# One decoder step on one core: layer norm's roots in one group, linear attention by split operands, sample columns turned in one piece, h's sums two per tile

## The reference, cut to what matters

```
a_u, a_v = gelu(a_u), gelu(a_v)
vn = layernorm(a_v)                       # per token, over 1024 channels
s  = spatial_mix(vn, w_s, b_s)            # 128x128 lower triangle, per head of 128 channels, per chunk of 128 tokens
out_a = a_u * s * silu(a_z)
# linear attention, 4 heads, keys of 128, values of 256
scores = where(mask, q_dec @ k_dec.T, 0)
o  = scores @ v + q_dec @ S               # S: state carried from chunk to chunk
S  = exp(b_last) * S + k_scaled.T @ v
out_b = rmsnorm(o) * gn_g * silu(b_z)
out_c = softmax(c_q @ mk.T / 16) @ mv * silu(c_z)
x = x + (sum over the branches: sigmoid(gate) * (out @ w_branch)) @ w_out
```

## Time and profile before

| | us |
|---|---|
| median of 3 runs | 867.17 (866.44 to 868.7) |
| the profiled execution | 868.86 |
| its span, first to last instruction | 866.6 |
| TensorE busy | 853.5 |
| VectorE busy | 430.2 |
| ScalarE busy | 377.3 |
| GpSimd busy | 92.4 |

### The profile page before, as it was taken

The page is one execution under the profiler, slowest core; times in us unless marked ns, Lnnn a source line. Parts: engine busy times, 40 slices in busy tenths (PEclk is TensorE's granted clock), DMA queues, the critical chain, the costliest instruction groups (busy, mean ns, idle before and its releaser), DMA issues.

```text
span 866.6 us, 16310 instructions
## 1 busy us (share of the span) xinstructions
PE 853.5 (98%) x6931; PEld 829.1 (96%) x6931; DVE 430.2 (50%) x748; ACT 377.3 (44%) x596; POOL 92.4 (11%) x127
## 2 busy tenths in 40 slices
PE   8999999999999999999999999999999999999997
PEld 8999999999999999999999998999989999999995
DVE  6525642634454466323337788545343544445634
ACT  7534445247555442422232275333234544534424
POOL 1001000000000222101012158000110000000000
PEclk9999999999999999999999999999999999999999
DMA  8325743331322659623366861425563341252402
GB/s 294 80 88 167 256 146 98 96 102 49 116 80 86 212 194 338 218 72 113 135 219 227 309 194 52 145 99 194 195 243 98 99 132 64 98 193 78 143 2 98
DMA packets 86067, 126.10 MB, mean 146 GB/s; under 512 B 3058, under 2 KB 72736, under 8 KB 86000
## 3 DMA queue, kind: packets, MB, share of 16 engines
q1 hardware_dynamic: 72288, 76.58, 27.1%
q0 software_dynamic: 13616, 48.48, 16.0%
q10 hardware_dynamic: 96, 0.06, 0.0%
HBM read 112.91 MB, written 12.19 MB: 144 GB/s over the span
## 4 chain that ended last, share of the span: by engine, by line
PE 95%; DVE 2%; ACT 1%; DMA 1%; issue 1%; ACTq 0%; DVEq 0%
PE mm L1020 63%; PE mm L981 5%; PE mm L994 5%; PE mm L970 3%; PE mm L1304 2%; PE mm L1230 2%; PE p L955 1%; PE p L957 1%; PE p L956 1%; PE mm L1251 1%; PE mm L1250 1%; PE mm L1249 1%; PE p L1189 1%; PE p L1159 1%; PE p L1133 1%; PE p L1130 1%
## 5 line engine op out<-in xcount | busy, mean ns | idle before, releaser
L1020 PE MATMUL mm<-h_lo,w_hi 128*128 128x260 f32 (+1 forms) x1088 | 223.6, 287 | 2.0 <-DVE w_lo L1399 2.0
L1020 PE MATMUL mm<-h_hi,w_hi 128*128 128x260 f32 (+1 forms) x1088 | 219.6, 283 | 0.0
L1020 PE MATMUL mm<-h_hi,w_lo 128*128 128x260 f32 (+1 forms) x1088 | 218.9, 283 | 0.0
L1399 DVE TENSOR_TENSOR w_lo<-raw,w_hi 128x1024 fp32r<-128x1024 f32 x130 | 159.4, 1229 | 89.2 <-ACT w_hi L526 88.0
L1020 PEld LDWEIGHTS mm<-h_lo,w_hi 128*128 128x128 f32 x1088 | 168.6, 189 | 6.2 <-issue 3.3
L1020 PEld LDWEIGHTS mm<-h_hi,w_lo 128*128 128x128 f32 x1088 | 168.1, 189 | 0.0
L1020 PEld LDWEIGHTS mm<-h_hi,w_hi 128*128 128x128 f32 x1088 | 168.1, 189 | 0.0
L526 ACT ACTIVATE w_hi<-raw 128x1024 fp32r<-128x1024 f32 x130 | 135.8, 1052 | 13.9 <-DMA raw<-in_w_mem_kv_dram 5.1
L1020 PE MATMUL mm<-x_lo,w_hi 128*128 128x260 f32 (+1 forms) x448 | 96.2, 284 | 0.0
L1020 PE MATMUL mm<-x_hi,w_hi 128*128 128x260 f32 (+1 forms) x448 | 95.3, 283 | 0.0
L1020 PE MATMUL mm<-x_hi,w_lo 128*128 128x260 f32 (+1 forms) x448 | 95.1, 282 | 0.0
(11 more groups left out here) (359 smaller groups left out, 1367.3 us busy)
## 6 DMA issues: line engine op xcount, KB each, us to landing
raw<-in_w_in_dram SPq DMA_DIRECT2D x44, 1024.0 KB, 5.3
raw<-in_w_branch_dram SPq DMA_DIRECT2D x12, 1024.0 KB, 5.2
raw<-in_w_mem_kv_dram SPq DMA_DIRECT2D x8, 1024.0 KB, 5.8
gate<-in_cache_mem_k_dram POOLq DMA_DIRECT2D x16, 512.0 KB, 6.2
tok<-in_cache_mem_v_dram POOLq DMA_DIRECT2D x14, 512.0 KB, 5.0
tok<-in_state_gla_dram POOLq DMA_DIRECT2D x8, 512.0 KB, 6.8
out_dram<-tok POOLq DMA_DIRECT2D x8, 512.0 KB, 6.9
work<-scr_q POOLq DMA_DIRECT2D x8, 512.0 KB, 5.1
```

The source lines that it names most:

```text
L1020: ins = MM(mm[:, j % 2, a, 0:c1 - c0], wp[:, j, k, :], xp[:, k, c0:c1], start=(k == 0 and wp is w_hi and xp is xl), stop=(k == KT - 1 and ...
L1399: V.tensor_tensor(w_lo[:, j], raw[:, j // 2, :, (j % 2) * P:(j % 2 + 1) * P], f32(w_hi[:, j]), ALU.subtract).then_inc(split_done, 1)
```

## The change

Four edits:

- **h's sums.** Two slices behind each of K's tiles 1 to 4, none behind the others.
- **Sample columns.** BV's, CQ's and AV's sample columns are written by ScalarE to `qsT` (samples by slices), turned by one transpose each (`rows_turn`), copied by VectorE to 64 rows (`rows8`) and stored by GpSimd to memory, from where they are read as 8 rows of 1024. The eight-row transposes in `to_tokens` and in PB's hook are gone.
- **Linear attention.** BV's values are no longer kept in `tok` but as `x_hi`, `x_lo`; scores and keys are split as well, and the products are made by `three`. The subtractions for `x_lo` read PSUM, so TensorE waits for them (`v_rows_lo`) before it writes the bank again, in BV and at BZ's first two tiles. The product with the state stays fp32.
- **Layer norm.** The statistics of four row blocks and of the samples are made first (`ln_stats`, AU's tiles 1 to 3), then ScalarE takes all roots in two instructions (`ln_roots`, tile 3), then VectorE inverts and scales block 0 (tile 3) and blocks 1 to 3 (tile 4); `samples_affine` moves to tile 5. What GpSimd does is the same.

The diff, cut to its core (declarations of buffers and of semaphores that follow from it are left out):

```diff
+        qsT = sb("qsT", [P, B, KT])
...
@@ -393,8 +404,8 @@
             pool.wait_ge(evac_done, first("V") + KT)
             pool.dma_start(v_prompt[0, 0].rearrange("(n p) h d -> p n (h d)", p=P), tok[:, 2:4, :]).then_inc(sem("kv_stored"), 16)
-            pool.wait_ge(tr_used, TR["BV"] + KT)
-            pool.dma_start(scr_v, stok[:, :]).then_inc(sem("vs_stored"), 16)
+            pool.wait_ge(sem("rows_up"), 1)
+            pool.dma_start(in_pieces(scr_v), rows8).then_inc(sem("rows_stored"), 16)
...
@@ -450,6 +462,11 @@
                     load_q(b)
                 src = cache_mem_k[0, i // 2].rearrange("(n p) h d -> p n (h d)", p=P)[:, i % 2, :]
                 pool.dma_start(kc[:, i % 4], src).then_inc(sem(f"ring_loaded{i % 4}"), 16)
+            pool.wait_ge(sem("rows_up"), 3)
+            pool.dma_start(in_pieces(scr_a), rows8).then_inc(sem("rows_stored"), 16)
+            pool.wait_ge(sem("rows_stored"), 48)
+            pool.dma_start(stok[:, :], scr_a).then_inc(sem("as_loaded"), 16)
...
@@ -602,15 +619,35 @@
                 for n in range(MT):
                     A(tok[:, 2 + n, cs], mm[:, j // 2, n, 0:2 * P], ACT.Copy).then_inc(evac_done, 1)
-            def evac_halves(name, it, j, g):
+            def evac_stage(name, it, j, g, f):
+                act.wait_ge(prod_done, g + j)
+                wait(act, tr_done, it * 4 + j + (TR[name] - 1))
+                for u in range(2):
+                    A(qsT[:, :, 4 * it + j - 1 + u], mm[:, u, 0, 256:TT - 256], f)
+                A(stage[:, 0, 0:256], mm[:, 0, 0, 0:256], f)
+                A(stage[:, 1, 0:256], mm[:, 1, 0, 0:256], f).then_inc(evac_done, 1)
+            def evac_gla_values(it, j, g):
+                c = 4 * it + j
                 if j % 2 == 0:
                     return
-                f = ACT.Gelu_apprx_tanh if name == "AV" else ACT.Copy
-                act.wait_ge(prod_done, g + j)
-                wait(act, tr_done, it * 4 + j + (TR[name] - 1))
-                A(stage[:, 0, 0:TT - 256], mm[:, 0, 0, 0:TT - 256], f)
-                A(stage[:, 1, 0:TT - 256], mm[:, 1, 0, 0:TT - 256], f).then_inc(evac_done, 1)
+                evac_stage("BV", it, j, g, ACT.Copy)
+                for u in (c - 1, c):
+                    act.wait_ge(tr_done, TR["BV"] + u + 1)
+                    A(x_hi[:, u, 256:T], p45[:, u % 2, 0:256], ACT.Copy).then_inc(sem("v_hi"), 1)
+                act.wait_ge(sem("rows0_done"), c // 2 + 1)
+                A(x_hi[:, c - 1:c + 1, 0:P], mm[:, 0, 1, 0:2 * P].rearrange("p (a b) -> p a b", b=P), ACT.Copy).then_inc(sem("rows0_out"), 1)
+                act.wait_ge(prod_done, g + j + 1)
+                A(x_hi[:, c - 1:c + 1, P:2 * P], mm[:, 1, 1, 0:2 * P].rearrange("p (a b) -> p a b", b=P), ACT.Copy).then_inc(evac_done, 1)
+            def evac_halves(name, it, j, g):
+                if j % 2 == 0:
+                    return
+                f = ACT.Gelu_apprx_tanh
+                evac_stage(name, it, j, g, f)
...
+                if 5 <= q < 5 + 3 * NT and q % 3 == 2:
+                    gla_split_hi((q - 5) // 3)
...
-                    act.wait_ge(sem("ln_mv"), 1)
-                    A(slstd, smv[:, 1:2], ACT.Sqrt, bias=eps_col[0:B, :]).then_inc(sem("ln_rt"), 1)
-                if name == "AU" and 2 <= c < NT + 2:
-                    ln_root(c - 2)
+                if name == "AU" and c == 3:
+                    ln_roots()
...
+            def gla_split_hi(n):
+                act.wait_ge(sem("sc_done"), n + 1)
+                A(ktk_hi[:, :, :], p45[:, 0, :].rearrange("p (h c) -> p h c", c=P), ACT.Copy).then_inc(sem("gla_hi"), 1)
+                act.wait_ge(sem("ssb_ready"), n + 1)
+                A(ssb_hi[:, :, :], ssb, ACT.Copy).then_inc(sem("gla_hi"), 1)
...
-            def ln_root(n):
-                act.wait_ge(sem("ln_mv"), n + 2)
-                A(lstd, mv[:, 1:2], ACT.Sqrt, bias=eps_col[:, :]).then_inc(sem("ln_rt"), 1)
+            def ln_roots():
+                act.wait_ge(sem("ln_mv"), NT + 1)
+                A(s_std, s_mean[:, 1:2], ACT.Sqrt, bias=eps_col[0:B, :]).then_inc(sem("ln_rt"), 1)
+                A(ln_std, ln_mean[:, :, 1:2].rearrange("p n c -> p (n c)"), ACT.Sqrt, bias=eps_col[:, :]).then_inc(sem("ln_rt"), 1)
...
@@ -989,6 +1037,8 @@
                             pe.wait_ge(sem("z_used"), 2 * BH)
                         to_tokens(name, it, j - 1, g)
                         to_tokens(name, it, j, g)
+                    if name == "BV":
+                        wait(pe, sem("v_rows_lo"), 4 * it + j - 1 + n - 1)
...
@@ -1000,6 +1050,8 @@
             def project(name, j, t):
                 pe.wait_ge(split_done, t + 1)
+                if name == "BZ" and t < first("BZ") + 2:
+                    pe.wait_ge(sem("v_rows_lo"), KT - 1 + t - first("BZ"))
...
@@ -1029,9 +1081,11 @@
                 n_rows = NT // 2 if name in HALVED else MT
                 for n in range(n_rows):
                     ins = TRP(p45[:, j % 2, n * P:(n + 1) * P], stage[:, j % 2, n * P:(n + 1) * P], ident[:, :])
-                if name in HALVED:
-                    ins = TRP(p67[0:B, j % 2, 0:P], stage[:, j % 2, 256:TT - 256], ident[:, :])
                 ins.then_inc(tr_done, 1)
+            def rows_turn(bank):
+                return TRP(bank[0:B * KT, 0:P], qsT[:, :, :].rearrange("p b k -> p (b k)"), ident[:, :])
...
@@ -1054,6 +1108,9 @@
                     b = c - 4 if name == "GB" else c + 4
                     sample_out(b)
                     sample_out(b + 1)
+                if name in BEHIND and c == 0:
+                    pe.wait_ge(evac_done, first(name))
+                    rows_turn(p67[:, 1, :]).then_inc(sem("rows_T"), 1)
...
-                    for k in range(KT):
-                        ins = TRP(p67_8[0:B, k, :], qsT[:, k, :], ident[:, :])
-                    ins.then_inc(sem("dq_T"), 1)
+                    rows_turn(p67[:, 0, :]).then_inc(sem("rows_T"), 1)
...
@@ -1119,18 +1174,20 @@
                 ins.then_inc(sem("sc_done"), 1)
             def gla_out(n):
-                pe.wait_ge(sem("ssb_ready"), n + 1)
                 if n >= 1:
                     pe.wait_ge(sem("ops_ready"), 2 * n + 2)
                     pe.wait_ge(sem("state_ready"), n)
+                if n == 0:
+                    pe.wait_ge(tr_used, TR["BV"] + KT)
+                pe.wait_ge(sem("gla_lo"), 2 * n + 2)
+                v = [[p[:, 2 * h:2 * h + 2, n * P:(n + 1) * P] for p in (x_hi, x_lo)] for h in range(BH)]
                 for h in range(BH):
-                    v = tok[:, n, h * BV:(h + 1) * BV]
                     if n >= 1:
                         MM(p67_4[:, h, :], eB[:, h, :], state[:, h, :], start=True, stop=False)
-                    ins = MM(p67_4[:, h, :], ssb[:, h, :], v, start=(n == 0), stop=True)
+                    ins = three(p67_4[:, h, :], (ssb_hi[:, h, :], ssb_lo[:, h, :]), v[h], n == 0, True)
                 ins.then_inc(sem("o_done"), 1)
                 for h in range(BH):
-                    ins = MM(p45_4[:, h, :], ktk[:, h, :], tok[:, n, h * BV:(h + 1) * BV], start=True, stop=True)
+                    ins = three(p45_4[:, h, :], (ktk_hi[:, h, :], ktk_lo[:, h, :]), v[h], True, True)
...
@@ -1409,8 +1466,20 @@
                     if name == "K":
                         V.tensor_copy(tok[:, 0:2, cs], src[:, 0:MT, :]).then_inc(tr_used, 1)
                     else:
-                        V.tensor_copy(stok[:, cs], p67[0:B, j % 2, 0:P]).then_inc(sem("stok_in"), 1)
-                        V.tensor_copy(tok[:, 2:4, cs], src[:, 0:2, :]).then_inc(tr_used, 1)
+                        if name == "BV":
+                            dve.wait_ge(sem("v_hi"), c + 1)
+                            V.tensor_tensor(x_lo[:, c, 256:T], p45[:, j % 2, 0:256], f32(x_hi[:, c, 256:T]), ALU.subtract).then_inc(tr_used, 1)
+                            if j % 2 == 1:
+                                for n in range(2):
+                                    if n == 0:
+                                        dve.wait_ge(sem("rows0_out"), c // 2 + 1)
+                                    else:
+                                        dve.wait_ge(evac_done, g + j + 1)
+                                    row = x_hi[:, c - 1:c + 1, n * P:(n + 1) * P]
+                                    V.tensor_tensor(x_lo[:, c - 1:c + 1, n * P:(n + 1) * P], mm[:, n, 1, 0:2 * P].rearrange("p (a b) -> p a b", b=P),
+                                                    f32(row), ALU.subtract).then_inc(sem("v_rows_lo"), 1)
+                        else:
+                            V.tensor_copy(tok[:, 2:4, cs], src[:, 0:2, :]).then_inc(tr_used, 1)
...
@@ -1444,10 +1513,11 @@
                         dve.wait_ge(sem("memT_hi"), k + 1)
                         V.scalar_tensor_tensor(out=x_lo[:, k, 0:MEM], in0=x_bank(X_M + k), scalar=gm1[:, k:k + 1],
                                                in1=f32(x_hi[:, k, 0:MEM]), op0=ALU.mult, op1=ALU.subtract).then_inc(sem("memT_lo"), 1)
```

(64 more changed lines are left out.)

59 lines of the change are left out of this document (34 added, 25 removed).

## The result

The changed kernel takes 869.85 us in the median of 10 runs (868.49 to 871.21), the kernel before 866.88 in 10 runs beside them (866.27 to 868.7): ratio 1.0029, 95% interval 1.0020 to 1.0038. By the ratio that is 2.5 us slower: clear of no change by its interval, and just inside the 0.3% that the prediction took as what a measurement can tell. Forecast were 869.6 us, with a chance of 0.43 for no change and of 0.39 for slower. The profiled execution took 869.89 us (span 867.8), the profiled one of before 868.86 (span 866.6).

What follows compares the result with a forecast made beforehand. TensorE, busy nearly the whole span, was taken as the bound: its work, gaps and clock. Terms -1.0 - 2.3 - 1.5 + 1.7 - 3.9 + 7.8 + 1.6 = +2.4 us gave 869.6 us; range 863.5 to 873.0.

Steps and rivals of the forecast that it cites:

- gets its turn only when VectorE's queue of operations with two SBUF inputs pauses: AU's layer norm: GpSimd's 2.3 us products are shut out by back-to-back VectorE operations, ending at 546.6; TensorE reaches mix(0) at 538.8.
- a second product of 5 us or more beside the three scales: Sign in AU: GpSimd's second layer-norm product stretches to 5 us or more while VectorE runs the three scales.
- The wait at mix(0) that I forecast: GA's start: TensorE waits 5 to 8 us for GpSimd's layer-norm products, priced at +7.8 us.
- The stall that goes, -3.9: AU: without a root per row block, ScalarE no longer holds tile 6's split; stall and half clock go, -3.9 us.
- Stall and clock, +7.8 and +1.6: GA's mix(0): TensorE waits 7.8 us for GpSimd's late products, then the slow clock stretch costs 1.6 us.
- Do the scales collide?: AU: whether ln_scale shuts GpSimd out; forecast yes, stall 7.8 us; rival no, stall 5.5, total 867.3, chance 0.20.
- BV's end, +1.7: BZ's first tile waits for VectorE's row subtractions, +1.7 us; rival that the clock falls there too: +1.6, 871.2, chance 0.14.
- The linear attention, -1.5: Split products instead of fp32 save 2.4 us, returns to fp32 cost 0.9: -1.5; rival that they save nothing: 871.1, chance 0.06.
- the +0.9 for returns between split and fp32: Linear attention, chunks 1 to 3: 9 more returns from split to fp32 matmuls at 0.1 us each, +0.9 us.
- Sample columns, -2.3: BV, AV and PB: 21 fewer transposes of 0.109 us each, after counting three new ones, -2.3 us.
- h's sums, -1.0: Sums done early in K: TensorE's wait of 0.8 us and about 0.2 of restarting go, -1.0 us.
- The base: Starting time for the sum: profiled execution 868.86 (span 866.6 and 2.3 around it), median of three runs 867.17, 1.7 lower.

Runs made afterwards that it cites:

- short products: GpSimd's eight layer-norm products cut to the first 8 of 1024 columns: on the changed kernel 862.06 us, ratio 0.9944; on the kernel before 864.19 us, ratio 0.9962.
- the scales spread: Changed kernel with one scale in each of AU's tiles 4, 5 and 6 and the samples' affine in tile 7: 868.52 us, ratio 1.0022.
- the row work first: Changed kernel with VectorE's evacuation work for BV's last tile ahead of later tiles' splits, head 2's sum and scan moved to tile 7: 867.83 us, ratio 1.0010.
- the sums alone: Kernel before with only h's sums changed, two per tile in K's tiles 1 to 4: 866.99 us, ratio 0.9994.

## Why the prediction was right, and which step of it was wrong

The time and the sign came out, and so did the theory that GpSimd's products and VectorE's operations hinder each other after the new layer norm. One step of the working was wrong in its mechanism and a second in its cause, and that the errors cancelled to 0.3 us was luck.

**The step that failed: "gets its turn only when VectorE's queue of operations with two SBUF inputs pauses".** I played the layer norm through with VectorE back to back and GpSimd shut out, and got a GpSimd that is 7.8 us late at mix(0) and "no wait on w_lo in AU". The prediction's own sign was a second product of 5 us or more beside the three scales; it took 2.74 (515.01). In the trace GpSimd gets every second turn, its eight products end at 538.5, and it is VectorE that is late, at w_lo for AU's tile 7 and for GA's first. I had generalised from one row: the product of 4.99 at 520.69, which waited out three operations of VectorE. In the changed kernel it happens once as well (533.55, 4.98), and at the same point of the program: behind the samples' second operation on 8 partitions. The other seven are turns. A row that spoke for turns was there too, the tile's product of 2.12 at 511.89, which waited out a product of GpSimd that had begun first, and so did the 3.31 at 518.38 (GpSimd's product ran from 517.24 to 520.61), an operation that takes 1.27 alone. (Two slips in the sums of that step are of no weight: eight times 2.3 is 18.4, not 18.6, and the turns as played add up to 546.4, not 546.6.)

Had VectorE not been late, TensorE would have come to mix(0) after 53.5 us of AU (that is what the kernel with short products takes, 482.53 to 536.03 in its chain), at 535.4, and would have waited there for GpSimd until 538.5. The wait at mix(0) that I forecast was thus not wrong in kind, but 3.1 us at most, and covered by the gaps on w_lo. With the scales spread it came to light.

**The stall that goes, -3.9.** It did go, but its cause was not the one that I named (ScalarE's root for each block). With short products it goes from the kernel before too, its roots untouched. This matters for what to do: without the products the order of the roots changes nothing (53.4 and 53.5 us), and the stall was the collisions' alone.

**Stall and clock, +7.8 and +1.6.** Measured: 1.61 - 0.12 = 1.5 and 4.81 - 0.12 = 4.7 us in two gaps, and 8.33 - 5.78 = 2.55 in the chain's first 48 matmuls of GA, together 8.75 against 9.4 (62.2 - 53.5 gives 8.7). AU from its start to mix(0) took 57.2 us before and 62.2 after: +5.0, against -3.9 + 7.8 + 1.6 = +5.5. The waits alone are 6.2 against 7.8, and the clock 2.55 against 1.6, so that the sum came so near is in part luck. For the rest I think that the excluded time is nearly the same whichever of the two engines waits; no run tests that.

**Do the scales collide?** Yes. Of the three in the row at 515.42 the first and the third take 2.88 each instead of 0.8, and end 0.55 after a product of GpSimd; the second takes 0.80: it had begun before GpSimd, whose next product needs the first scale's result, was ready again (0.63 idle ahead of 518.38). So the value that the rows left open, and for which I took the higher price, holds. The Trainium skill (SBUF — State Buffer, "Who interferes with whom") names tensor_scalar among the operations that can take the shared pair, and the trace agrees. The same section says that whichever engine issues first has the pair for its whole instruction and the other fully blocks; the trace agrees with that as well (w_lo at 521.74, blocked for 2.2 us), and it was this rule, not mine, that pointed to a late VectorE. One row does not fit it: GpSimd's product of 533.55 began before the split of 534.48 and yet waited it out, and the product of the tile behind it.

**Why the old order was less bad.** In the kernel before, the two statistics operations of a row block stand beside a product of GpSimd (513.54 to 516.28). From the timeline of VectorE in the kernel before:

```profile
514.14 1.41 DVE L1694 BATCH_NORM_STATS2 small<-tok 128x6 f32<-128x512 f32 x2
```

The same pair takes 1.40 with no product beside it, at 507.01. Statistics don't collide here. The old order had one block's statistics, aggregate and root (some 2.2 us) in each of four tiles, three of them with products about, in which GpSimd could work for free. The new one does them all before GpSimd's first product and leaves it only company that collides. This reading is from the rows; no run moved the statistics alone.

**BV's end, +1.7.** 1.8 in the trace; 1.6, give or take 1.1, by the run with the row work first. Right in place, size and mechanism. The clock did not fall behind it.

**The linear attention, -1.5.** -2.3: TensorE's stretch from the first scores to the last product is 95.68 us before and 93.40 after. The term that was off is the +0.9 for returns between split and fp32. Per head, the fp32 product and the three split ones take 0.78 = 0.43 + 0.35 in the chain; the border costs nothing. The difference of 5.95 and 5.73, from which I took its price, belongs to the 48 matmuls behind the scores and is there after as well (5.94 and 5.77).

**Sample columns, -2.3.** BV and AV are each 0.88 shorter and PB 0.74, and the new transpose in BZ takes 0.11: -2.4. (The one in AU is in AU's figure.)

**h's sums, -1.0.** V begins 0.9 us earlier (chain: 93.11 before, 92.20 after), as forecast. In the changed kernel's profile nothing takes it back. With the sums alone 0.5 us of it are left by the ratio, and the profile shows TensorE waiting a few microseconds later for weights that are not there yet; the interval holds the whole 0.9 as well. I had looked at the next operation of VectorE behind the sums, not at the next transfer.

**The base.** The terms as measured are -0.9 - 2.4 - 2.3 + 1.8 + 5.0 = +1.2; the spans differ by 867.8 - 866.6 = 1.2. I had +2.4. The time still came out, for a reason that I had not seen: the profiled execution of before was 1.7 to 2.0 us above the median, and I carried this distance over. In the changed kernel the profiled execution and the median are the same. The kernel before has runs in which the clock falls and runs in which it does not. In its profile TensorE is at the lower level for 3.4 us at two places before the span's end: from 523.48, behind the gap in AU, and from 8.07, behind a gap of 2.13 in which TensorE waits for a load. Of the second, the timeline of TensorE and a window (length, busy us, granted clock, DMA share, GB/s):

```profile
7.69 0.23 PE L1323 MATMUL mm<-ident,stage 46*128 46x46 f32 x1 [1.86 <-DMA stage<-in_b_g_dram]
8.00:11.60 3.60, 3.60 (x19) 0.53 1.05 390
```

Of its 17 runs beside one of the experiments, six with a mean granted clock of 0.999 took 866.3 to 866.7 us, five with 0.997 took 867.8 to 868.1, and six with 0.995 or 0.996 took 868.65 to 869.2. A fall of 3.4 us to half is 0.002 of such a mean, so I read the three groups as neither fall, one and both; these runs have no profile of their own. The step between the first two, 1.5 us, fits the 1.6 that the fall in AU costs in the windows. The changed kernel's ten runs all have 0.993 to 0.996. So the sum was 1.2 too high, the base 1.7 too low, and the part of an execution outside its span 0.2 shorter than the 2.3 that I carried over (869.89 - 867.8 = 2.1).

## What to carry to other kernels

When work is split between VectorE and GpSimd, count GpSimd's products with SBUF inputs as time in which VectorE's two-input operations and scales stand still, and look which engine has something urgent behind them; here moving 26.8 us of the changed kernel's GpSimd work to VectorE, where it takes 10, made VectorE more punctual and the kernel 8.6 us faster than the changed one (ratios 0.9930 and 1.0029), 6 us faster than the one before. Before taking a dependency out of such a stretch ask what the other engine did in its pauses: operations that don't collide (statistics) may be what keeps it in time. And check whether a gap's cause is the one next to it in the order of waits: leaving out the neighbour's work, on the kernel before, would have shown it in one run.
